# Experts' weight refills split over two queues in a two-block model kernel

## The chip, the cores and the metric

The kernel runs on one core of one Trainium2 chip. The metric is the device time of one execution in microseconds; the lower, the better. Three runs of the kernel before gave 1797.9, 1798.71 and 1805.41 us, median 1798.71.

## What is computed

The reference is a model of two blocks over 256 tokens of width 1024: a first block of two layers (convolution and attention mixing, memory attention, MLPs), and a second one with an RWKV-7 mixer, a Mamba-2 mixer, and a mixture of experts. Only the last part matters here. Every token is routed to the best of four groups and to two of the eight experts within it:

```python
def run_block(args):
    tok, e = args
    xb = ht[tok]
    hid = jax.nn.silu(xb @ w_gate[e]) * (xb @ w_up[e])
    return hid @ w_down[e]
```

with `w_gate` and `w_up` of 1024 x 512 and `w_down` of 512 x 1024 for each of 32 experts, all float32, 2 MB each. The weighed results are added to the tokens, and a last RMS norm closes the model.

## The kernel before

All stages before the experts have been done when the span is at about 1340 us; the experts' stage takes the rest. It runs over all 32 experts, whatever the routing, with 64 token slots for each. `experts_stage` writes the program of each engine by hand; the engines meet by counting semaphores.

**Weights.** The 96 matrices are units 0 to 95 in the order gate, up, down of expert 0, then of expert 1, and so on. There are ten slots of 2 MB in SBUF, four of `weight_slots` and six of `moe_slots`; unit n goes to slot n % 10. Units 0 to 9 are loaded before the stage. Each later one waits until the unit that was in its slot ten places earlier is used up. The loop at the end of SyncE's program does that for all of them: with `e, kind = divmod(n - n_slots, 3)`, a slot of kind 0 or 1 (it held a gate or an up matrix of expert e) is refilled when `grown` has reached e + 1, one of kind 2 (it held a down matrix) when `lowered` has reached e + 1. As ten isn't a multiple of three, unit n = 10 + 3e + kind is another sort of matrix than the one it replaces: kind 0 gets an up matrix, kind 1 a down matrix, both of expert e + 3, and kind 2 the gate matrix of expert e + 4.

**TensorE** (`expert` in the tensor program) does for each expert: the growth, 32 matmuls with the gate and the up matrix in turn (line 3309, counts `grown`), after it has waited for both of them to have landed; the scatter of the expert before (3300); the transposes of the grown bank (3316), once ScalarE has copied it; the gathering of the next expert's tokens (3280) and of its selection (3288); and the product with the down matrix (3326, counts `lowered`).

**ScalarE** does three things for each expert: it copies the grown bank to SBUF (3346, on `grown`), applies Silu to the turned gate half (3348), and copies the result, weighed, as `y_hi` (3351, on `lowered`). Experts 0 to 23 are a hardware loop of three trips with eight experts in its body, experts 24 to 31 are written out behind it. **VectorE** multiplies the halves, selects the next tokens and makes `y_lo` (3401), in a loop of the same form.

Of the kernel before, what the change touches and what calls it, by code (L numbers as in the profile page):

```python
# [69 lines left out]
NE, NG, EPG, DE = 32, 4, 8, 512  # L70
# [190 lines left out]
def program(nc, a, out, at, dumps=()):  # L261

    with ExitStack() as ctx:
# [42 lines left out]
        def c_(name):  # L306
            lo, hi = at[name]
            return const[:, lo:hi]
# [14 lines left out]
        stream = Stream(slots, [ctx.enter_context(nc.semaphore(f"weights_landed_{s}")) for s in range(RING)])  # L323
# [365 lines left out]
        for tile, group in enumerate(rows_of):  # L689
            r = 0  # L690
            for name, v in group:
                size = int(np.prod(v.shape))
                n = size // P
# [20 lines left out]
        def everywhere(v, n, off=0):  # L714

            return bass.AP(v.tensor, v.offset + off, [[0, P], [1, n]])
# [2494 lines left out]
        def experts_stage(h_tok, rank_col, more, landed_more, gate_parts, eye, rows_stored, final_row, final_landed,  # L3211
                          stored, flag, late_flags):

            def load_flag(name, eng):
                late_flags[name] = eng.value_load(flag[0:1, 0:1], min_val=0, max_val=P)  # L3215


            u0 = unit["moe"]
            assert u0 % RING == 0
            body = 8  # L3220
            trips = NE // body
            n_slots = RING + MORE
            nm = DE // P
            with ExitStack() as on:
# [25 lines left out]
                def slot(n):  # L3250

                    s = n % n_slots
                    return slots[:, s, :] if s < RING else more[:, s - RING, :]
# [4 lines left out]
                def landed(n):  # L3258

                    s = n % n_slots  # L3260
                    return stream.sems[s] if s < RING else landed_more[s - RING]
# [7 lines left out]
                with meeting() as block:  # L3269
# [70 lines left out]
                    @block.scalar  # L3340
                    def _(act):
                        load_flag("act", act)

                        def expert(i, b):
                            act.wait_ge(grown, i * body + (b + 1))
                            act.activation(grown_sb[:, :], ps[:, 0], ACT.Copy).then_inc(grown_out, 1)  # L3346
                            act.wait_ge(turned, i * body + (b + 1))
                            act.activation(opened_sb[:, :, :], turned_gate, ACT.Silu).then_inc(opened, 1)  # L3348
                            act.wait_ge(lowered, i * body + (b + 1))
                            act.wait_ge(spread_ready, i * body + (b + 2))  # L3350
                            act.activation(y_hi[:, :], ps[:, 3], ACT.Copy, scale=slot_gate[:, b % 2, :]).then_inc(y_out, 1)  # L3351

                        act.activation(y_hi[:, :], c_("noughts"), ACT.Copy).then_inc(y_out, 1)
                        with act.Fori(0, trips - 1) as i:
                            for b in range(body):
                                expert(i, b)
                        for b in range(body):
                            expert(trips - 1, b)
                        last_scalar(act)

                    @block.vector
# [59 lines left out]
                    @block.sync  # L3421
                    def _(sp):
                        stream.prefetch(sp, u0)
                        load_flag("sp", sp)
                        sp.dma_start(final_row[:, :], everywhere(a["final_norm_g_2"], D)).then_inc(final_landed, 16)
                        sp.wait_ge(rows_stored, 16)

                        for n in range(n_slots, 3 * NE):
                            e, kind = divmod(n - n_slots, 3)
                            sp.wait_ge(lowered if kind == 2 else grown, e + 1)  # L3430
                            sp.dma_start(slot(n), stream.src[u0 + n][0]).then_inc(landed(n), 16)
                        last_sync(sp, stored)


# [301 lines left out]
```

## Time and profile before

| | |
|---|---|
| runs, median | 1798.71 us (1797.9 to 1805.41) |
| profiled execution, device time | 1807.74 us |
| its span, first to last instruction | 1806.0 us |
| mean granted TensorE clock | 0.974 of full speed |
| TensorE busy, whole span | 1678.2 us (93%) |
| ScalarE busy, whole span | 601.1 us (33%) |
| experts' stage | about 1340 to 1799 us |
| mean DMA rate, whole span | 210 GB/s |
| DMA rate in the experts' stage | 425 to 428 GB/s in most slices |

The times of the profile are microseconds from the start of the span. A DMA share is the mean busy share of the core's 16 DMA engines; "landing" is the time from a DMA's issue to its completion. The queue q1 is that of the DMAs which SyncE issues, q10 that of ScalarE's, q0 GpSimd's, and q8 carries instructions to the engines. "SPq" and "ACTq" rows are the issues themselves, as the engine's queue spends time on them.

### The profile page before, as it was taken

Reading aid. Unit: us, or ns where it says so; the run is one execution under the profiler, and the core shown is the slowest. Engines: PE = TensorE matmul, PEld = TensorE weight load, DVE = VectorE, ACT = ScalarE, POOL = GpSimd, SP = SyncE. Lnnn points to the kernel's source line nnn. Section 1 sums busy time; section 2 is a strip of 40 time slices with the busy share of each in tenths; the row PEclk is TensorE's granted clock in tenths of the full one; section 3 lists DMA queues with packets and bytes.
Section 4 is the critical chain, followed back from the end, with each engine's and each line's share of the span. In section 5 each row is a group of like instructions: output and inputs, shape, how many; then the busy total and the mean of one; then the engine's idle time right before and its main releaser. Section 6 shows DMA issues by size and latency. Waiting matters only on the chain. (4 is left out here: it accounts for less than half of the span.)

```text
span 1806.0 us, 31150 instructions
## 1 busy us (share of the span) xinstructions
PE 1678.2 (93%) x13373; PEld 1197.8 (66%) x13373; DVE 917.1 (51%) x1468; ACT 601.1 (33%) x879; POOL 31.5 (2%) x47
## 2 busy tenths in 40 slices
PE   7989999898799998998889899989979999999996
PEld 4877888765578887988887895567744444444442
DVE  2566555424965555887765776645642212111212
ACT  1426444213754444342003664544321111111111
POOL 2000000000000000020000000000000000000000
PEclk9999999998999999998999999999989999999999
DMA  8245554242075553520002441442689999999994
GB/s 321 94 187 187 187 186 163 93 149 94 1 271 195 186 186 117 185 76 14 4 3 95 170 163 66 163 173 84 239 341 421 426 426 427 427 428 427 426 428 187
DMA packets 102042, 379.94 MB, mean 210 GB/s; under 512 B 9996, under 2 KB 20479, under 8 KB 89371
## 3 DMA queue, kind: packets, MB, share of 16 engines
q1 hardware_dynamic: 101360, 377.89, 53.9%
q8 instruction: 100, 1.64, 0.4%
q14 instruction: 27, 0.22, 0.0%
q0 software_dynamic: 352, 0.15, 0.0%
q10 hardware_dynamic: 203, 0.04, 0.0%
HBM read 376.92 MB, written 1.14 MB: 209 GB/s over the span
## 5 line engine op out<-in xcount | busy, mean ns | idle before, releaser
L3309 PE MATMUL ps<-moe_slots,moe_h 128*64 128x512 f32 x592 | 155.0, 593 | 3.3 <-DMA moe_slots<-in_w_exp_up 3.3
L1512 DVE TENSOR_TENSOR mlp_w_lo<-weight_slots,mlp_w_hi 128x2048 fp32r<-128x2048 f32 x60 | 134.8, 2289 | 40.9 <-ACT mlp_w_hi L1476 40.9
L3394 DVE TENSOR_TENSOR moe_hidT<-moe_silu,ps 128x256 f32<-128x256 f32 x32 | 13.5, 421 | 233.1 <-ACT moe_silu L3348 233.1
L1476 ACT ACTIVATE mlp_w_hi<-weight_slots 128x2048 fp32r<-128x2048 f32 x60 | 111.5, 1907 | 39.2 <-PE ps L138 39.2
L3309 PE MATMUL ps<-weight_slots,moe_h 128*64 128x512 f32 x432 | 120.8, 598 | 3.7 <-DMA weight_slots<-in_w_exp_up 1.7
L3309 PEld LDWEIGHTS ps<-moe_slots,moe_h 128*64 128x64 f32 x592 | 51.1, 137 | 85.0 <-issue 85.0
L138 PE MATMUL ps<-mlp_w_hi,mlp_hid_lo 128*128 128x512 f32 x256 | 99.9, 390 | 0.0
L137 PE MATMUL ps<-mlp_w_lo,mlp_hid_hi 128*128 128x512 f32 x256 | 99.9, 390 | 0.0
L136 PE MATMUL ps<-mlp_w_hi,mlp_hid_hi 128*128 128x512 f32 x256 | 99.7, 389 | 0.0
L1436 PE MATMUL ps<-mlp_h_far,mlp_w_hi 128*128 128x512 f32 x256 | 91.9, 399 | 0.0
L1436 PE MATMUL ps<-mlp_h_near,mlp_w_hi 128*128 128x512 f32 x256 | 90.8, 397 | 0.0
L384 PE MATMUL ps<-const 128*128 128x512 bf16 x280 | 70.4, 401 | 19.4 <-PEq L293 19.4
L3346 ACT ACTIVATE moe_grown<-ps 128x512 f32<-128x512 f32 x32 | 19.1, 598 | 205.5 <-PE ps L3309 205.5
L3309 PEld LDWEIGHTS ps<-weight_slots,moe_h 128*64 128x64 f32 x432 | 39.1, 138 | 67.7 <-issue 66.9
L3401 DVE SCALAR_TENSOR_TENSOR moe_y_lo<-ps,moe_slot_gate,moe_y_hi 128x512 fp32r<-128x512 f32 x32 | 24.0, 751 | 112.1 <-ACT moe_y_hi L3351 112.1
L3351 ACT ACTIVATE moe_y_hi<-ps,moe_slot_gate 128x512 fp32r<-128x512 f32 x32 | 22.0, 687 | 152.1 <-PE ps L3326 152.1
L1434 PE MATMUL ps<-mlp_h_far,mlp_w_lo 128*128 128x256 f32 x256 | 71.8, 280 | 0.0
L3326 PE MATMUL ps<-moe_slots,moe_hidT 128*64 128x512 f32 x304 | 69.4, 598 | 1.0 <-DVE moe_hidT L3394 1.0
L384 PEld LDWEIGHTS ps<-const 128*128 128x128 bf16 x280 | 26.7, 102 | 55.8 <-issue 31.1
L2803 PE MATMUL ps<-weight_slots,hT 128*128 128x512 f32 x128 | 63.6, 620 | 0.0
L671 PE MATMUL ps<-weight_slots,hT 128*128 128x512 f32 (+2 forms) x160 | 60.2, 538 | 2.5 <-PEq L293 1.9
L136 PE MATMUL ps<-xbc_h_hi,xbc_w_hi 128*128 128x256 f32 x192 | 54.9, 286 | 4.5 <-DVE xbc_w_lo L2661 4.5
(653 smaller groups left out, 4127.4 us busy)
## 6 DMA issues: line engine op xcount, KB each, us to landing
weight_slots<-in_w_in SPq DMA_DIRECT2D x20, 2048.0 KB, 7.8
moe_slots<-in_w_exp_up SPq DMA_DIRECT2D x19, 2048.0 KB, 23.6
moe_slots<-in_w_exp_down SPq DMA_DIRECT2D x19, 2048.0 KB, 27.2
moe_slots<-in_w_exp_gate SPq DMA_DIRECT2D x18, 2048.0 KB, 26.6
weight_slots<-in_w_up SPq DMA_DIRECT2D x16, 2048.0 KB, 8.3
weight_slots<-in_w_down SPq DMA_DIRECT2D x16, 2048.0 KB, 7.7
weight_slots<-in_w_exp_gate SPq DMA_DIRECT2D x14, 2048.0 KB, 25.1
weight_slots<-in_w_exp_up SPq DMA_DIRECT2D x13, 2048.0 KB, 21.6
```

What stands on the lines that cost most here:

```text
L136: pe.matmul(dst, left[0], right[0], start=start, stop=False, skip_group_check=inside)
L137: pe.matmul(dst, left[0], right[1], start=False, stop=False, skip_group_check=inside)
L138: return pe.matmul(dst, left[1], right[0], start=False, stop=stop, skip_group_check=inside)
L384: pe.matmul(ps[:, bank], nought[:, 0:P], nought[:, 0:UC], start=True, stop=True)
L671: mm = pe.matmul(dst, h[:, k, t * P:(t + 1) * P], w[:, k, c0:c0 + width], start=(first and k == 0), stop=(last and k == kc - 1))
L1434: pe.matmul(ps[:, m, 0:S], lo, h_part(k)[:, 0:S], start=False, stop=False, skip_group_check=True)
L1436: mm = pe.matmul(ps[:, m], hi, h_part(k), start=(k == 0), stop=(k == KD - 1), skip_group_check=True)
L1476: act.activation(piece_slot(w_split[0], jj), raw_piece(jj), ACT.Copy).then_inc(w_hi, 1)
L1512: dve.tensor_tensor(piece_slot(w_split[1], jj), raw_piece(jj), piece_slot(w_split[0], jj).bitcast(F32), ALU.subtract).then_inc(w_lo, 1)
L2803: mm = pe.matmul(z_bank(g, t), hT[:, k, t * P:(t + 1) * P], w[:, k, :], start=(k == 0), stop=(k == KD - 1))
L3309: mm = pe.matmul(ps[side(kind), 0, :], h_sel[:, k, :], w[kind][:, k, :], start=(k == 0), stop=(k == KD - 1))
L3326: mm = pe.matmul(ps[side(h), 3, :], hid_T[:, f, :], w_down[:, f, h * UC:(h + 1) * UC], start=(f == 0), stop=(f == nm - 1))
```

## The change

The refills of kind 2 (the slots that held down matrices) move from SyncE's program to ScalarE's. There each stands behind the `y_hi` copy of the same expert, which has waited for `lowered`. SyncE's loop keeps kinds 0 and 1. Since the unit's number is fixed when the program is built, ScalarE's loop of three trips becomes 32 experts written out. 28 refills move: units 12, 15, ... 93, the gate matrices of experts 4 to 31. TensorE's, VectorE's and GpSimd's programs stay as they are.

```diff
@@ the scalar program of experts_stage
+                        def refill(e):
+
+                            n = n_slots + 3 * e + 2
+                            if n < 3 * NE:
+                                act.dma_start(slot(n), stream.src[u0 + n][0]).then_inc(landed(n), 16)
+
                         act.activation(y_hi[:, :], c_("noughts"), ACT.Copy).then_inc(y_out, 1)
-                        with act.Fori(0, trips - 1) as i:
+                        for i in range(trips):
                             for b in range(body):
                                 expert(i, b)
-                        for b in range(body):
-                            expert(trips - 1, b)
+                                refill(i * body + b)
                         last_scalar(act)
@@ the sync program
                         for n in range(n_slots, 3 * NE):
                             e, kind = divmod(n - n_slots, 3)
-                            sp.wait_ge(lowered if kind == 2 else grown, e + 1)
-                            sp.dma_start(slot(n), stream.src[u0 + n][0]).then_inc(landed(n), 16)
+                            if kind < 2:
+                                sp.wait_ge(grown, e + 1)
+                                sp.dma_start(slot(n), stream.src[u0 + n][0]).then_inc(landed(n), 16)
```

## Rows read from the trace of the kernel before

**Rows 1.** Windows: stretch, length, busy us of each engine, PEclk, DMA share, GB/s.
```profile
1380.00:1480.00 100.00, 100.00 (x838) 45.10 (x838) 20.20 (x60) 15.23 (x25) 0.00 (x0) 1.00 1.01 427
...
1710.20:1724.90 14.70, 13.91 (x112) 6.37 (x114) 2.72 (x8) 1.68 (x4) 0.00 (x0) 1.00 1.00 426
...
1739.50:1755.00 15.50, 13.97 (x112) 6.43 (x114) 2.73 (x8) 1.71 (x4) 0.00 (x0) 1.00 1.00 426
```

**Rows 2.** Timeline of ScalarE: start, us, line, operation, [idle before <- releaser].
```profile
1359.96 0.69 ACT L3351 ACTIVATE moe_y_hi<-ps,moe_slot_gate 128x512 fp32r<-128x512 f32 x1 [4.59 <-PE ps L3326]
1366.75 0.60 ACT L3346 ACTIVATE moe_grown<-ps 128x512 f32<-128x512 f32 x1 [6.10 <-PE ps L3309]
...
1456.44 1.28 ACT L3346 ACT_TABLE_LOAD   x1
...
1463.14 1.28 ACT L3348 ACT_TABLE_LOAD   x1
...
1681.40 0.60 ACT L3346 ACTIVATE moe_grown<-ps 128x512 f32<-128x512 f32 x1 [6.10 <-PE ps L3309]
```

**Rows 3.** Timeline of SyncE's queue: the issues of units 10, 12, 88, 93 and 95.
```profile
1353.12 0.33 SPq L3431 DMA_DIRECT2D weight_slots<-in_w_exp_up  x1
...
1359.88 0.33 SPq L3431 DMA_DIRECT2D weight_slots<-in_w_exp_gate  x1
...
1710.16 0.33 SPq L3431 DMA_DIRECT2D moe_slots<-in_w_exp_up  x1
...
1731.67 0.33 SPq L3431 DMA_DIRECT2D weight_slots<-in_w_exp_gate  x1
...
1739.89 0.43 SPq L3431 DMA_DIRECT2D moe_slots<-in_w_exp_down  x1
```

**Rows 4.** Landings, one issue each: those of 1353.12, 1710.16, 1731.67, 1739.89; last is us.
```profile
weight_slots<-in_w_exp_up SPq DMA_DIRECT2D x1, 2048.0 KB, 8.3
...
moe_slots<-in_w_exp_up SPq DMA_DIRECT2D x1, 2048.0 KB, 37.5
...
weight_slots<-in_w_exp_gate SPq DMA_DIRECT2D x1, 2048.0 KB, 41.4
...
moe_slots<-in_w_exp_down SPq DMA_DIRECT2D x1, 2048.0 KB, 42.8
```

**Rows 5.** Waits of TensorE from 1344 us: us in total, times, longest.
```profile
PE ps L3309 <- DMA moe_slots<-in_w_exp_up: 4.7, 5, 1.5
PE ps L3309 <- DMA weight_slots<-in_w_exp_up: 1.7, 2, 0.9
```

**Rows 6.** Chain that ended last, in order of time: start, us, what.
```profile
1739.52 38.32 DMA moe_slots<-in_w_exp_up
...
1777.97 7.09 PE ps L3309 x32
1785.06 1.14 PE ps L3300 x8
```

**Rows 7.** Start of the kernel: three issues (start, us), and the landings of two.
```profile
1.25 0.45 SPq L779 DMA_DIRECT2D const<-in_const  x1
...
4.24 0.36 ACTq L805 DMA_DIRECT2D table<-in_rel_bias  x1
...
4.88 8.69 SPq L788 DMA_DIRECT2D gains<-in_b_q_gain  x1
...
const<-in_const SPq DMA_DIRECT2D x1, 1192.0 KB, 15.6
...
table<-in_rel_bias ACTq DMA_DIRECT2D x1, 1.5 KB, 6.5
```

**Rows 8.** DMA queues from 1360 to 1770 us: packets, MB, share of 16 engines.
```profile
DMA packets 12013, 175.12 MB, mean 427 GB/s; under 512 B 1324, under 2 KB 1324, under 8 KB 1324
...
q1 hardware_dynamic: 11986, 174.69, 100.2%
q8 instruction: 25, 0.41, 0.4%
```

## The prediction

> **What bounds the kernel now.** I read the table of windows first. From 1380 to 1480 us, and in every stretch up to about 1680, TensorE is busy the whole time at a granted clock of 1.00, while the DMA share is 1.01 at 427 GB/s: both are full at once. From about 1690 it is different: in the window from 1710.2 TensorE is busy for 13.91 of 14.70 us and the DMA share is still 1.00 [rows 1]. So the experts' stage has two clocks. TensorE alone takes 13.68 us an expert: ScalarE's copy of the grown bank starts at 1366.75 for expert 1 and at 1681.40 for expert 24, (1681.40 - 1366.75) / 23 [rows 2]. The stream of weights takes longer. The first refill (unit 10) is issued at 1353.12 and lands 8.3 us later, at 1361.4; the last (unit 95) is issued at 1739.89 and lands 42.8 us later, at 1782.7 [rows 3, 4]. That is 85 loads in 421.3 us, 4.956 us a load, 14.87 us an expert. The ten slots filled beforehand hide the deficit for some 25 experts; then TensorE waits for each "up" matrix, 4.7 + 1.7 us in seven waits [rows 5]. The chain of waits ends the same way: the up load of expert 31 issued at 1739.52 lands 38.32 us later, and the growth that it releases runs from 1777.97 to 1785.06 [rows 6]. With no lateness of the stream that growth would have ended at about 1366.7 + 30 x 13.68 = 1777.1. So the stream costs 8.0 us now, and no change to it can win more than that.
>
> One thing about names: the refill of a freed down slot (kind 2) does not carry a down matrix. Units are counted gate, up, down, and there are ten slots, so the unit put there is 12, 15, 18 and so on: the gate matrix of expert e + 4. The first one is the issue at 1359.88 [rows 3]. The SP queue now serves up, down, gate, up, down, gate: exactly the order in which TensorE will want them.
>
> **The change part by part.**
>
> *SP loses 28 waits on "lowered" and 28 issues* (0.33 us each, the row at 1359.88 [rows 3]). Nothing waits for them; SP only sleeps longer until the next "grown". Worth 0.
>
> *ScalarE gains 28 issues.* The issue stands behind the y_hi copy, which starts at 1359.96 and takes 0.69 us; the SP issue stood at 1359.88 [rows 2, 3]. So a gate is asked for some 0.8 us later. It joins a stream that is 35 to 40 us behind at the end, and the first time it still finds units 10 and 11 in front (issued from 1353.12 on, 9.9 us of work), so the DMA engines don't run dry: 0. Queued behind the issue on ScalarE is the copy of the next grown bank, for which TensorE waits. It starts at 1366.75; the queue is idle from 1360.65 on, 6.1 us [rows 2]. The price of an issue is 0.33 to 0.43 us for a transfer of this shape [rows 3]. The far end is 8.69 us, which SP's issue at 4.88 us took at the start of the kernel [rows 7]; that would put 2.6 us on each expert. I take 0.4, since the transfers are of the same shape and the ScalarE queue would hold one or two of them where SP's now holds up to nine without being held up. Covered: 0.
>
> *The loop written out.* The two table loads at each trip's start (1.28 us, the rows at 1456.44 and 1463.14) fall away for the second and third trip; both lie in idle time of ScalarE today [rows 2]: 0. The code grows by some 24 experts of about ten instructions, about one more 16 KB instruction packet. The trace has 25 of those from 1360 to 1770, 0.4% of 16 engines, so 1.05 us each on one of 16 engines [rows 8]: at most 1 us, I take 0.
>
> *The order in which loads land.* This is the part that counts. Gates now travel in a queue of their own beside the up and down matrices. What does the DMA do with two queues that both have work? The trace shows it in two places. The instruction packets (q8) take 1.05 us each; the 16 KB packets of q1 take about 100.2% x 16 x 410 / 10,662 = 0.62 us (the 11,986 packets less the 1,324 that are tiny); so a foreign packet waits for about one packet of q1 and not for the loads queued there [rows 8]. And at the kernel's start a ScalarE issue at 4.24 us lands 6.5 us later, while SP's const load, issued at 1.25, needs 15.6 us [rows 7]. So the engines take turns packet by packet, and a gate beside a busy SP queue gets half the stream: it lands in about 2 x 4.956 = 9.9 us and a few us of latency after its issue, where it now takes 41.4 us [rows 4]. But it isn't needed before 41 us. What it takes, it takes from up and down matrices that are needed first.
>
> The Trainium skill, page "DMA: Bandwidth & Descriptors", section "Queues, rings and completion order", states that each engine goes round robin between queue rows at the granularity of a packet. The rows above agree as far as they go; by a strict order of issue instead the sum below would be 0.
>
> *The sum.* The engines stay busy, so a matrix lands later than now by 4.956 us for each gate that has overtaken it. TensorE can't end before any "landing of up(e), plus the experts from e to the end at 13.68 us each".
> - Up 31: both remaining gates are in front of it in either order. It lands at 1777.8 as now.
> - Up 30: gate 31 has overtaken it. Now 1762.9 (14.87 before up 31), then 1767.9; plus 13.68 = 1781.6 for the start of expert 31.
> - Up 29: issued 1710.16, lands 37.5 us later at 1747.7 [rows 3, 4]. Gates 30 and 31 are both in front of it: gate 31 is issued when expert 27's down product is done, one period before up 29 is needed, and half the stream carries it in 9.9 us. 1747.7 + 9.9 = 1757.6; plus 2 x 13.68 = 1784.9.
> - Up 28: 14.87 earlier, 1732.8; two gates in front, 1742.7; plus 3 x 13.68 = 1783.7. Earlier ones give less, about 1.2 us for each expert (14.87 - 13.68).
>
> The latest is up 29. Expert 31 starts at about 1785.1 instead of 1777.97: **+7.1 us**. After it nothing is changed (last product, last scatter, closing norm, store). The first wait for an up matrix moves forward by about eight experts (9.9 us of overtaking at 1.2 us an expert), from about 1690 to about 1580; the waits are of 1.2 us, and such waits leave the granted clock at 1.00 today [rows 1].
>
> Against the profiled execution: span 1806.0 us and 1.7 around it, 1807.7; plus 7.1 is 1814.8. The runs' median is 1798.7, 9 us under the profiled one, and I carry the difference over: **1798.7 + 7.1 = 1805.8 us**, 0.4% more. About 0.5%, 9.0 us, is what a measurement of this kernel can tell from no change, so a true loss of 7.1 counts as within it.
>
> **The rivals.**
>
> *A. No overtaking.* If descriptors are served in order of issue whatever the queue, or if the runs without a profiler aren't bound by the stream, nothing happens: 1798.7. For it: the 9 us between profile and median are about the 8.0 us that the stream costs. If a load takes 4.86 us there, before just touches TensorE's floor (8.0 / 85 = 0.094 us less), and the change still costs about 7; at 4.77 us (15.1 / 80 = 0.19 less) it costs nothing. Against: the rows on instruction packets. The skill's section "Issuing engines are not separate DMA queues" on the same page says that several issuing engines only save the time to issue; taken alone, that is this rival. Chance 0.17.
>
> *B. Two queues carry less than one (slower).* Both queues have work for 2 x 4.956 of every 14.87 us, 2/3 of the 80 loads in front of up 29, 264 us. Each per cent lost there costs 2.6 us on top of 7.1. It decides from 0.7% on, where the total passes 9.0. The far row is the DMA at the start (rows of several queues, small pieces), no measure for 16 KB packets; the near one is the instruction packets, after which q1 goes on at full share. At 2%: 7.1 + 5.3, 1811.1. Chance 0.20, and that of a smaller share than 1/3 for ScalarE's queue, where gates would come too late, is within it.
>
> *C. Two queues carry more.* If the change of queue hides a gap, 2.7% (7.1 / 264) would cancel the loss, and the floor is 8.0 us under the present time: 1790.7, -0.45%. Against: the DMA share is already 1.00 to 1.01 with one queue [rows 1, 8]. Chance 0.06.
>
> **How the numbers follow.** My forecast, turn by turn at an unchanged rate: 0.57, 1805.8 us, alone 1802 to 1809. Of it some 0.10 falls over 9.0 us, since three runs of before spread from 1797.9 to 1805.4. The range of all: the low end is rival A less some spread, 1798; the high end rival B at 3% (7.1 + 7.9, 1813.7) and a little, 1815. Faster by over 0.5% is out of reach by any mechanism here and stays at 0.04 for a shift of the base; slower by over 0.5%: 0.10 + 0.19, and 0.01 for a ScalarE issue that is held, 0.30; within: 0.66.
>
> **What would show it.** In the profile after, gates issued by ScalarE should land in 11 to 14 us instead of 41; up matrices in the late part should land about 5 to 10 us later than before; the waits of TensorE's growth for an up load should start near 1580 us instead of 1690, with a sum near 14 us instead of 6.4; the last one or two experts should run at 13.7 us without a wait, and the down matrix of expert 31 should still land near 1782.7. If gates still need about 40 us, it is A. If down 31 lands later by several us with a DMA share of 1.00, it is B; earlier, C. Waits of the transposes for the grown copy would show a held ScalarE. The forecast is wrong above all if the stream isn't the bound in ordinary runs.

## The result

The changed kernel took 1809.92 us (median of 8 runs, 1807.45 to 1814.85), the kernel before 1801.34 us (8 runs, 1797.9 to 1805.75). The ratio is 1.0044, 95% interval 1.003 to 1.0059: 5.4 to 10.6 us slower. The loss is clear of the noise and small.

The profiled execution of the changed kernel has a span of 1808.0 us, only 2.0 more than that of before. That is because the two reached the experts' stage at different times. From here on I measure the stage by itself: from the start of ScalarE's copy of expert 1's grown bank to the start of that of expert 31. Before, that was 1366.75 to 1785.10 (rows of that kind are in [rows 2]; 1785.10 is 0.04 after the end of the growth in [rows 6]), 418.35 us. ScalarE's timeline of the changed kernel:

```profile
1361.63 0.60 ACT L3346 ACTIVATE moe_grown<-ps 128x512 f32<-128x512 f32 x1 [6.18 <-PE ps L3309]
...
1573.74 0.69 ACT L3351 ACTIVATE moe_y_hi<-ps,moe_slot_gate 128x512 fp32r<-128x512 f32 x1 [4.73 <-PE ps L3326]
1573.75 0.33 ACTq L3357 DMA_DIRECT2D weight_slots<-in_w_exp_gate  x1
1581.26 0.60 ACT L3346 ACTIVATE moe_grown<-ps 128x512 f32<-128x512 f32 x1 [6.83 <-PE ps L3309]
...
1759.72 0.60 ACT L3346 ACTIVATE moe_grown<-ps 128x512 f32<-128x512 f32 x1 [7.92 <-PE ps L3309]
...
1787.11 0.60 ACT L3346 ACTIVATE moe_grown<-ps 128x512 f32<-128x512 f32 x1 [6.18 <-PE ps L3309]
```

The stage is 1787.11 - 1361.63 = 425.48 us, 7.13 more than before. TensorE's waits, all for up matrices, answer to [rows 5]:

```profile
PE ps L3309 <- DMA moe_slots<-in_w_exp_up: 7.8, 8, 1.5
PE ps L3309 <- DMA weight_slots<-in_w_exp_up: 4.3, 5, 1.5
```

Thirteen waits of 12.1 us in place of seven of 6.4: 5.7 us. The rest is in the growth itself, which takes 7.10 us after such a wait and 6.87 without one: six more of them, 6 x 0.23 = 1.4. The chain, in order of time, has the same two lengths:

```profile
1714.90 37.56 DMA moe_slots<-in_w_exp_up
...
1752.60 7.09 PE ps L3309 x32
...
1780.20 6.87 PE ps L3309 x32
```

The chain of before left the stream at up 31, the last up matrix [rows 6]. This one leaves it at up 29, landed at 1752.46, and TensorE's own work of 13.69 us an expert sets everything behind it. The landings of single issues say how that came about. Here are gate 31, up 31 and down 31, in the form of [rows 4]:

```profile
weight_slots<-in_w_exp_gate ACTq DMA_DIRECT2D x1, 2048.0 KB, 14.8
...
moe_slots<-in_w_exp_up SPq DMA_DIRECT2D x1, 2048.0 KB, 27.9
...
moe_slots<-in_w_exp_down SPq DMA_DIRECT2D x1, 2048.0 KB, 33.1
```

Gate 31, issued at 1736.43, is there at 1751.2, just before up 29 and 29 us before its use at 1780.2. Down 31, the last load of all (issued 1744.65), lands at 1777.7, 416.1 us after the stage's start; before it was 1782.7 - 1366.75 = 415.95. The stream as a whole is as fast as before. The queues from 1360 to 1770 us answer to [rows 8]:

```profile
DMA packets 12026, 175.15 MB, mean 427 GB/s; under 512 B 1335, under 2 KB 1335, under 8 KB 1335
...
q1 hardware_dynamic: 7993, 116.43, 66.8%
q10 hardware_dynamic: 4006, 58.30, 33.5%
```

How two busy queues share the engines can be read directly. The gate issued at 1573.75 has none of its 16 KB packets on an engine before 1577.0, 3.3 us after its issue. Its 2.10 MB then pass from 1577 to 1587 us, beside SyncE's queue:

```profile
q1 hardware_dynamic: 150, 2.20, 51.6%
q10 hardware_dynamic: 143, 2.10, 49.2%
```

The two queues get half each. Gate 31 gives the same picture from 1740 to 1750 (51.2% and 48.8%), and its first microsecond shows the grain: in five windows of 0.3 us from 1739.6 on, the engines work for q1 alone, q10, q10, q1, q1. They change over about every 0.6 us, the time of one 16 KB packet in the prediction.

### The profile page after: what moved, and what is told of

Its sections match the earlier page's. It is cut to its first block and busy times, and to the rows that moved or that the text cites. A ratio compares the mean times of both kernels' runs of the same rounds, so it can differ in the third digit from the quotient of the medians.

```text
span 1808.0 us, 31115 instructions
## 1 busy us (share of the span) xinstructions
PE 1673.7 (93%) x13353; PEld 1196.1 (66%) x13373; DVE 916.8 (51%) x1468; ACT 594.3 (33%) x874; POOL 31.4 (2%) x47
## 6 DMA issues: line engine op xcount, KB each, us to landing
moe_slots<-in_w_exp_gate ACTq DMA_DIRECT2D x16, 2048.0 KB, 14.8
```

## The experiments

Theory: gates in a queue of their own overtake up and down matrices that are needed first; nothing else costs anything. Rivals: each issue on ScalarE costs time; two queues carry less than one; the written-out loop costs time. For each kernel I give the stage as above, since the time of whole runs scatters by 8 to 10 us. Each stage is that of one profiled execution. No kernel was profiled twice, so how well a stage repeats is not measured: the differences of 3 us and more carry the argument, and a stage that is off by less than 1 us is read as next to no change.

Five kernels ran only once, so their whole time says little by itself: first sixteen gates 1803.9 us, last twelve gates 1808.8, down matrices 1812.7, up matrices 1806.1, late gates issued 6.8 us earlier 1804.2; the kernel before had medians of 1802.1 to 1803.9 beside them. The order is that of the stages.

**All refills on ScalarE.** ScalarE issues kinds 0 and 1 behind the grown copy and kind 2 behind y_hi; SyncE's loop is gone.

```diff
                             act.activation(grown_sb[:, :], ps[:, 0], ACT.Copy).then_inc(grown_out, 1)
+                            refill(i * body + b, 0)
+                            refill(i * body + b, 1)
...
-                                refill(i * body + b)
+                                refill(i * body + b, 2)
```

> All 86 refills are issued by ScalarE, in the old order of units (after each grown copy the refills of kinds 0 and 1, after each y_hi that of kind 2); SyncE issues none, and the loop is written out. One queue, so nothing can overtake. Overtaking as the cause: from ScalarE's second grown copy to its last 418.3 us as in the kernel before (418.35), 7.1 less than in the changed one (425.48); time within 0.1% of before. Rival, that issuing from ScalarE or the written-out loop costs the time: 28 issues cost 7.1, so 86 cost 20 us or more, and the stage takes over 435.

Stage 418.74 us (1362.00 to 1780.74), 0.4 over before; time ratio to before 0.9986 (0.9971 to 1.0), no loss. Its queue row from 1360 to 1770 us is that of [rows 8] under another name:

```profile
q10 hardware_dynamic: 11985, 174.68, 100.2%
```

So 86 issues on ScalarE and the written-out loop together cost no more than about 0.4 us of stage. Both rivals of that sort fall.

**Which gates do the harm.** The changed kernel with `n < 60` or `n >= 60` as a further condition for ScalarE's refill; the others go back to SyncE.

> Only the gates of units 12 to 57 (16 of 28) are issued by ScalarE, the last 12 by SyncE. Overtaking: what gates gained early has been given back by the time the stream binds, +0.1 us on the stage of before (418.4). Rival, a cost for each issue or a slower stream while two queues work: 16/28 of 7.1, +4.1 (422.4).

> The complement: only the gates of units 60 to 93 (12 of 28) are issued by ScalarE. Overtaking: the whole loss is in the last ones, +7.1 us (425.4). Rival, a cost for each issue or of the stream with two queues: 12/28 of 7.1, +3.0 (421.4).

Stages: 418.95 with the first sixteen gates on ScalarE, +0.6, and 425.69 with the last twelve, +7.3. Sixteen overtaking gates cost next to nothing and twelve cost all of it. The sixteen do make TensorE wait, for experts 16 and 17, but after that no growth waits until expert 26. A price per issue, or a stream slowed while two queues work, would have shared the loss 16 to 12. It is as with a debt: what an early gate takes is given back when that gate's turn in the old order comes, and the stage pays only for gates that are ahead when TensorE runs out of slack.

**Which matrix overtakes.** ScalarE's issues, 29 in either kernel, are those of kind 1 (down matrices) or of kind 0 (up matrices), behind the grown copy, and SyncE keeps the two other kinds.

> ScalarE issues the refills of kind 1 (down matrices of expert e + 3, after the grown copy) and SyncE those of kinds 0 and 2. A down matrix is the last one needed of its expert, so overtaking costs more: 9.5 to 11 us over the stage of before (428 to 429.3), worked through load by load. Rival, a cost for the mere use of ScalarE's queue: 7.1 as in the changed kernel (425.5), since the number and size of its issues are the same.

> ScalarE issues the refills of kind 0 (up matrices of expert e + 3). An up matrix is needed together with its gate, which now comes later; overtaking costs less: 5 to 6 us over before (423.3 to 424.4), and the waits of the growth are for gates instead of up matrices. Rival: 7.1 again (425.5).

Down matrices ahead: 428.08, +9.7. Up matrices ahead: 422.29, +3.9, less than the 5 to 6 expected; the sign and the order of the three cases (down, gate, up: 9.7, 7.1, 3.9) are as worked out, the size of the last one is 1.1 off and I did not settle why. As expected, its growths no longer wait for up matrices. TensorE's longest row reads:

```profile
PE ps L3309 <- issue: 8.6, 7, 3.3
```

The profile puts these waits down to nothing that it shows. The landings settle it: SyncE's issue of gate 22 at 1600.56 lands 46.7 us later, at 1647.3, and the growth of expert 22, after the longest wait of 3.3 us, starts at 1647.36. It waited for its gate.

**Taking the stream's limit away.** A pair: in both kernels a down refill brings only half of its columns, and the result is not that of the reference.

```diff
-                            sp.dma_start(slot(n), stream.src[u0 + n][0]).then_inc(landed(n), 16)
+                            if n % 3 == 2:
+                                sp.dma_start(slot(n)[:, 0:2 * D], stream.src[u0 + n][0].rearrange("(p k) c -> p (k c)", p=P)[:, 0:2 * D])\
+                                    .then_inc(landed(n), 16)
+                            else: ...
```

> The kernel before, but the refill of each down matrix brings only the first half of its columns in every partition (the other half keeps old values, so the result of the experts isn't that of the reference): the stream needs 5/6 of 14.87 us an expert, 12.4, less than TensorE's 13.68. No wait for the stream is left: stage at 30 x 13.68 = 410.4 us, 8.0 less than before, time ratio about 0.9956. Control for the next one.

> The changed kernel with the same halved down refills. Overtaking: an order of landing costs nothing where the stream isn't the bound, so the stage is 410.4 us too, and the time that of the control. Rival, a cost on ScalarE or of two queues by itself: it stays, 417 us and 7 us over the control.

Stages 410.54 (before's order) and 410.42 (changed): no wait for a load is left in either, and the changed order costs nothing. That also confirms the 8.0 us put on the stream: 418.35 - 410.54 = 7.8. The times of whole runs are less sharp: ratios to before 0.9945 (0.9927 to 0.9964) and 0.997 (0.9955 to 0.9986). The two intervals overlap.

**Two queues, no overtaking.** From unit 60 on, ScalarE issues each gate two experts later.

```diff
-                            n = n_slots + 3 * e + 2
-                            if n < 3 * NE:
-                                act.dma_start(...)
+                            for n in (n_slots + 3 * e + 2, n_slots + 3 * (e - 2) + 2):
+                                late = n != n_slots + 3 * e + 2
+                                if n < 3 * NE and late == (n >= 60):
+                                    act.dma_start(slot(n), stream.src[u0 + n][0]).then_inc(landed(n), 16)
```

> As the changed kernel, but from unit 60 on each gate is issued by ScalarE two experts later, after y_hi of expert e + 2: two queues, the same number of ScalarE issues, but a gate comes just in time and overtakes almost nothing. Overtaking: worked through load by load with two queues at half the stream each, the stage is 0.1 us longer than before (418.5). Rival, that two queues or the issues cost the time by themselves: 425.5 as in the changed kernel. Rival, that gates are asked for too late here: over 425.5, with waits for gate loads.

Stage 421.33: +3.0, neither the 0.1 nor the 7.1. The time of whole runs, ratio 1.0008 (0.9993 to 1.0023), can't tell 3 us from none. Two rows of its trace, of TensorE's waits and of the landings:

```profile
PE ps L3309 <- issue: 7.1, 10, 1.1
...
weight_slots<-in_w_exp_gate ACTq DMA_DIRECT2D x9, 2048.0 KB, 15.0
```

A gate needs 15.0 us to land (the median of the twelve late ones too, 13.8 to 15.4), and from its issue to the growth that needs it there is one expert's period of 13.7, so the gate itself became the late one: gate 31, issued at 1763.11, lands 14.7 us later at 1777.8, and its growth starts at 1777.97. A further kernel issues it 6.8 us earlier, behind the grown copy of expert e + 2:

> As the kernel with gates two experts late, but 6.8 us earlier: from unit 60 on a gate is issued by ScalarE behind the grown copy of expert e + 2, 20.5 us before the growth that needs it. In the kernel with the late gates the stage was 421.3 instead of 418.5; gates landed in 14 to 15 us, more than the 13.7 they had. If that was the miss, no growth waits for a gate here, and a gate overtakes only what 6.8 us at half the stream bring: +0.8 to 1.6 us over before, load by load, at most the 2.2 of the rule of thumb (3.4 - 1.2): 419 to 420.6. If two queues cost something of their own: 421 to 422 again.

Stage 419.14, +0.8, with 28 issues on ScalarE and two queues at work throughout; the growth waits for up matrices alone again (5.0 us in seven waits). When a gate comes in time and hardly overtakes, the loss is gone. So two queues cost at most the 0.8 us.

One growth of this kernel shows something else, a fall of the clock. Its row, and a window of 2 us inside it (the figure before the last two is the granted clock):

```profile
1731.36 8.78 PE L3309 MATMUL ps<-moe_slots,moe_h 128*64 128x512 f32 x32 [2.01 <-DMA moe_slots<-in_w_exp_up]
...
1733.00:1735.00 2.00, 2.00 (x6) 0.61 (x4) 0.00 (x0) 0.00 (x0) 0.00 (x0) 0.50 1.02 434
```

TensorE had waited 2.0 us, the granted clock went to 0.50, the lower of its two levels (1.2 GHz), and this growth took 1.7 us longer than the 7.09 of others after a wait. The kernels with the last twelve gates, with the down and with the up matrices on ScalarE have one such growth of 8.78 or 8.79 us each, after waits of 2.5, 1.95 and 3.3 us. A wait of 1.98 us in the kernel with all refills on ScalarE and one of 2.02 in that with the down matrices were not followed by it. None of this lengthened a stage much, since a later growth of each of the four still waited for its load and took the delay up.

**Can the stream's own 8 us be won?** In the trace of before the stream stands still at the stage's start: the slots of the first growth are freed only when it ends, at about 1353.0, and by then the ten loads ahead have landed. A window of it (the last two figures are the DMA share and the GB/s):

```profile
1352.00:1354.00 2.00, 2.00 (x14) 0.81 (x10) 0.00 (x0) 0.91 (x2) 0.00 (x0) 1.00 0.00 0
```

From 1350 to 1354 the share is at most 0.06 in any microsecond. Of the 5.9 us that the next expectation reckons as standing still, only these 4 are idle engines; from 1354 to 1356 they are busy at 270 GB/s.

Three kernels refill the slots of a gate and an up matrix piece by piece while the growth that reads them still runs. A growth goes through eight parts of either matrix, the "k columns" 0 to 7. TensorE signals after some of them, and SyncE then sends that part of the refill. Quarters for expert 0:

> The kernel before with one step against the stream's start: the first two refills (units 10 and 11) go out in four quarters each, as the growth of expert 0 is done with the k columns 0 and 1, 2 and 3, 4 and 5, 6 and 7. In the kernel before the last load of the first ten has landed at about 1350.6 us and the first refill lands at 1361.4, 10.8 us later where 4.956 would do: the stream stands still for 5.9 us. If the stream's total time is what the stage ends by, the quarters fill about 5 us of that: first wait for an up matrix about four experts later, stage about 413.3 us, and 5 us less time, ratio 0.997. Rival, that the end is set by TensorE or by the order alone: 418.3.

Stage 417.68, -0.7, ratio 0.9995 (0.9983 to 1.0008). The expected 5 us didn't come. I blamed the small pieces, since this window shows engines busy at a low rate (4 KB pieces):

```profile
1345.00:1350.00 5.00, 5.00 (x72) 3.28 (x72) 1.51 (x4) 2.26 (x3) 0.00 (x0) 1.00 0.94 306
```

> As the kernel with quarters, but the first two refills go out in halves, the first ones after the k columns 0 to 3 of expert 0's growth, some 3.5 us before its end. The quarters gained 0.7 us of 5: units 10 and 11 in 4 KB pieces kept the DMA engines 94% busy for 306 GB/s. If the size of the pieces was what ate the gain, 8 KB pieces (0.97 busy at 384 GB/s in the kernels with halved down loads) keep about 3 of 3.5 us: stage 415.4. If a start of the stream ahead of its time brings nothing: 418.3.

Stage 417.52, -0.8, ratio 0.999 (0.9977 to 1.0003): larger pieces brought next to nothing more, so the size was not what ate it. The landings show where at least part of it went. Unit 11, counted from the end of the first growth, landed after 10.6 us instead of 13.2, but unit 13 after 21.5 instead of 23.1:

```profile
weight_slots<-in_w_exp_down SPq DMA_DIRECT2D x1, 1024.0 KB, 10.2
...
1366.28 0.33 SPq L3443 DMA_DIRECT2D weight_slots<-in_w_exp_up  x1
...
weight_slots<-in_w_exp_up SPq DMA_DIRECT2D x1, 2048.0 KB, 7.8
```

Unit 13 lands 7.8 us after its issue, where it took 9.4 before, and 6.0 us after unit 12, where it was 4.9 before: the stream had run short of work until expert 1's growth freed the next slots. Of the 2.6 us, 1.0 was lost there, and by unit 16 only 0.8 was left. With halves for experts 0, 1 and 2:

```diff
+                                if i == 0 and b < 3 and k == 3:
+                                    mm.then_inc(eaten, 1)
...
+                            if e < 3 and kind == 0:
+                                for q in range(2):
+                                    sp.wait_ge((eaten, grown)[q], e + 1)
+                                    cols = slice(q * 4 * UC, (q + 1) * 4 * UC)
+                                    for m in (n, n + 1):
+                                        flat = stream.src[u0 + m][0].rearrange("(p k) c -> p (k c)", p=P)
+                                        sp.dma_start(slot(m)[:, cols], flat[:, cols]).then_inc(landed(m), 16)
...
```

> With halves for expert 0 alone, unit 11 landed 2.6 us and unit 12 2.6 us earlier against the end of the first growth, but unit 13 only 1.6 and the last one 0.8: the stream had caught up with its own supply, as unit 13 may not be asked for before expert 1's growth is done. Here the refills of kinds 0 and 1 of experts 0, 1 and 2 go out in halves. If supply at the start is the limit, the 2.6 us are kept, less a few tenths for the 8 KB pieces: stage 415.8 to 416.3, ratio about 0.9987. If not, 417.5 again.

Stage 416.68 (1358.21 to 1774.89), -1.7, a little short of the expected 415.8 to 416.3; time 1798.06 us against 1801.81, ratio 0.9981 (0.9965 to 0.9997). Of the 3.7 us between the medians the stage shows 1.7; the rest is within the scatter. It is the only kernel with the reference's result whose interval lies below that of no change, and by little.

## Why the prediction was right, point by point

*The bound.* The step that the stream costs 8.0 us and TensorE's floor lies right under it held: 7.8 with the stream's limit taken away.

*SyncE's part, the loop, ScalarE's issues at 0.* Held; with 86 issues on ScalarE the stage was 0.4 us longer. One detail was wrong without consequence: I let the issue start after the y_hi copy, 0.8 us later than SyncE's. The row at 1573.75 starts 0.01 us after the copy's start. The issue itself takes 0.33 to 0.37 us, as taken from [rows 3].

*Turns packet by packet.* Held. The rows that I took it from were thin: the time that a packet takes says nothing of how long it queued, and the ScalarE load at the start was one of 1.5 KB. The changed kernel shows it: 51.6% to 49.2% while a gate is under way, in turns of about 0.6 us. From 1360 to 1770 the two queues together fill the engines at 427 GB/s, and gates land in 14.8 us (median; 12.6 to 15.6). I had said 11 to 14. The 9.9 us at half the stream were right (1577 to 1587); the latency of "a few us" was 4.9, of which 3.3 pass before the first data and the rest behind the last. That did not enter this sum (up 29 still found gate 31 in front, by 1.3 us), but it is what made the gates late in the kernel that issues them two experts later. By the Trainium skill, "DMA: Bandwidth & Descriptors", section "Queues, rings and completion order", the engines go round robin; this trace agrees, with 14.8 us for a gate in place of 41.4 [rows 4].

*The sum.* Up 29 was to be the latest and to land 9.9 us later than before: it landed 1752.46 - 1361.63 = 390.8 us into the stage, before 1747.7 - 1366.75 = 380.9, so 9.9 us later. Expert 31 was to start 7.1 us later: 7.13. That the two agree to a few hundredths is luck. The prediction's own sum ends at 1784.9, which is 6.9 us after 1777.97 and not the 7.1 written there, and it leaves out that the growth of expert 29, too, takes 0.23 us longer after its wait; in the measured 7.13 that is in. Nothing behind it changed; the last two experts ran at 13.7 us without a wait, and down 31 landed when it had before. The waits began at 1574, about the 1580 foretold; their sum was 12.1 where I said near 14, the difference being the slower growth after a wait.

*Rival A* (no overtaking) rested on the 9 us between the profiled execution and the median. That gap was not the stream's. The profiled executions of the twelve kernels here reach the second grown copy at 1358.2 to 1366.3 us, before's at 1366.75: its execution was late before the stage began. The granted clock goes with it: executions of before with a mean granted clock of 0.978 or 0.979 took 1797.4 to 1802.4 us, those at 0.972 or 0.973 took 1806.9 to 1808.2, and the profiled one had 0.974 and took 1807.74. Where ahead of the stage the clock was lower I did not look into.

*Rivals B and C* (two queues carry less, or more) fall by the 427 GB/s and by the 416.1 us to the last landing.

*The absolute time.* The forecast was 1805.8, the measurement 1809.9. That is inside the range of all cases, 1798 to 1815, and 0.9 us above the range that I gave this case alone, 1802 to 1809. Of the difference 2.6 us is the base: its median went from 1798.7 with three runs to 1801.3 with eight. What is left, 8.6 us of difference between medians against 7.1, is inside the interval of 5.4 to 10.6.

## What to carry to other kernels

When loads are the bound and one queue issues them in the order of their use, a second queue doesn't add bandwidth, it changes the order: while both have work, half the engines' time goes to whatever stands in it, however late that is needed. Before moving loads to another queue, ask for each one what it will overtake, and weigh it at the last point where the compute engine still has no slack; overtaking that is given back before that point is free. If the issuing engine must change, move the whole ordered stream (+0.4 us here), or issue the moved loads just early enough for their landing time at half the rate (+0.8 us here).

## What the runs showed that I had not expected

- An issue that stands behind an activation in ScalarE's program starts 0.01 us after the activation does, not at its end (0.69 us later).
- Beside a full queue a 2 MB load takes 14.8 us to land, not the 9.9 of half the stream's rate and the 3.3 us that the first refill took beyond its 4.96 (8.3 - 4.96).
- A growth whose weights came late takes 7.10 us instead of 6.87 once it has started, with the granted clock at 1.00. Four growths, after waits of 1.95 to 3.3 us, took 8.78 us with the clock at 0.50 for a part of them.
- Starting an idle stream earlier gains only as long as the next loads can be asked for earlier too: 2.6 us won at unit 11 had shrunk to 1.6 at unit 13 and to 0.8 at the end.
